# Seven products in place of eight over 1024 rather than 512 inner rows of six down projections

## The chip, the cores and the metric

One core of one Trainium2 chip runs the whole program. The metric is the device time of one execution in microseconds (us). GB/s and MB are decimal; a load of 512 KB is 0.524 MB.

## The reference, cut to what matters

Two layers work on 256 tokens of width 2048: a mixer each (attention with a window beside a gated recurrence, then stick-breaking attention), and after each mixer an MLP. The change touches the MLPs alone.

```python
def squared_relu_mlp(hn, w_up, w_down):            # hn: 256 x 2048
    return jnp.square(jax.nn.relu(hn @ w_up)) @ w_down   # w_up: 2048 x 8192, w_down: 8192 x 2048
...
h = h + squared_relu_mlp(rms_norm(h, norm_mlp[layer]), w_up[layer], w_down[layer])
```

## The kernel before

Every operand of the large matmuls is float32, split into two parts that TensorE takes at its fast rate: ScalarE writes the rounded part (`w_hi`), VectorE the rest (`w_lo` = raw - `w_hi`), and a product of two operands x and w is three matmuls, x_hi·w_hi, x_hi·w_lo and x_lo·w_hi.

Weights come in pieces of 512 KB over SyncE's queue into a ring `raw` of four slots, and their two parts go into a ring `w_split` of four slots. ScalarE splits piece v once it has landed and once TensorE is through with piece v-4; VectorE follows (`lo_done`), and then TensorE may take piece v and SyncE may load piece v+4. ScalarE and VectorE run three pieces ahead (`AHEAD = 3`): at step s of a quad or a pair they split piece s+3, and at its last three steps the first three pieces of what comes next. Each engine keeps to its written order, so an instruction that waits holds up all behind it.

An MLP is four chunks of 2048 hidden units. A chunk has four up quads (eight pieces each, 128 matmuls; four tiles of hidden units) and then the down projection of the chunk's 2048 inner rows to the 2048 output columns. When two tiles of an up quad are complete (after pieces 3 and 7) the drain `hidden` takes them: a copy `cross` on ScalarE, `total` and `relu_sq` on VectorE, a split into `ff_op` by both. In the last chunk of each layer the down projection is four plain wide quads.

In the other three chunks of each layer, six in all, it is two pairs, p = 0 and p = 1, of 1024 output columns each. A pair is an output of two row halves (tokens 0 to 127 and 128 to 255) by two column halves of 512 (n = 0, 1). A piece of a pair is (n, s): 256 inner rows s by 512 columns. Plainly it gives two products of six matmuls, one for each row half. The first two row blocks (s = 0, 1) of both column halves make a 2 by 2 by 2 block product, and it is done with seven products in place of eight, with sums of x (`x_sum`, made once a chunk) and of weights (`w_sum`). So a pair has 31 products, 186 matmuls: 24 plain ones of 12 pieces, one each of the four pieces of the block, three of sums (after pieces 5, 7 and 8). The weight sums are four VectorE instructions (`w_sum_t1`, `w_sum_t3_t2`, `w_sum_t4`) and one more copy of a piece that SyncE loads.

In `pair_dve`, VectorE does at step s: the part `w_lo` of piece s+3, then what belongs to the step; `pair_add` adds a PSUM bank, scaled by 1/rms, into `h`. Four of the eight adds come early in the pair, because an intermediate product has to go into two quarters of the output and its bank is used again.

GpSimd issues four DMAs of 512 KB and a few small ones in the first mixer, and does nothing in the MLPs.

Of the kernel before, what the change touches and what calls it, by code (L numbers as in the profile page):

```python
# [29 lines left out]
F32 = mybir.dt.float32  # L30
F32R = mybir.dt.float32r
# [5 lines left out]
P = 128  # L37
# [8 lines left out]
GC = 256  # L46
# [4 lines left out]
SPLIT_SLOTS = 4  # L51

# [46 lines left out]
def build(nc, x, rel_bias, norm_mix, even_w_in, even_conv_w, even_conv_b, even_gate_a_w, even_gate_a_b,  # L99
# [30 lines left out]
    with ctx:  # L130
# [26 lines left out]
        rstd_tok = rstd_all[:, S:S + TB]  # L157
        ident = sb("ident", [P, P])
# [135 lines left out]
        w_copy_in, w_sums, w_sum_hi, w_sum_lo = sem("w_copy_in"), sem("w_sums"), sem("w_sum_hi"), sem("w_sum_lo")  # L294
# [363 lines left out]
        def norm_sum(dve, n):  # L658

            dve.wait_ge(sq_done_tok, 8 * (n + 1))  # L660
            if n % 2:
# [6 lines left out]
                dve.wait_ge(rstd_done, n + 1)  # L668
                return
# [724 lines left out]
        SUM_AT = (0, 1, 0)  # L1394

        def after_pair(Q, v):

            return 10 * Q + (v + 1 if v < 9 else 11 if v == 9 else v + 2 if v < 15 else 20)

        def after_pair_half(Q, n, tb):  # L1400

            return 10 * Q + (10 + tb if n == 0 else 17 + 3 * tb)

        def pair_banks(p):

            return 1 + 2 * p, 2 * p, 2 - 2 * p, 3 - 2 * p

        def load_pair(sp, Q, w, row, col, T):

            for v, (n, s) in enumerate(PAIR):  # L1410
                slot = v % RAW_SLOTS
                if v not in (AT_B11, AT_B21):
                    sp.wait_ge(lo_done, 8 * Q + (v + 1 if v + 1 in (AT_B11, AT_B21) else v) - RAW_SLOTS + 1)
                src = w[bass.ds(row + s * 2 * P, 2 * P), bass.ds(col + n * 2 * GC, 2 * GC)].rearrange("(t p) n -> p t n", p=P)
                sp.dma_start(rows_512(raw[:, slot]), src).then_inc(raw_in[slot], 16)
                if v == AT_B11:
                    src = w[bass.ds(row, 2 * P), bass.ds(col + 2 * GC, 2 * GC)].rearrange("(t p) n -> p t n", p=P)
                    if not (isinstance(T, int) and T == 0):
                        sp.wait_ge(w_sum_lo, 3 * T - 1)
                    sp.dma_start(w_sum[:, 1], src).then_inc(w_copy_in, 16)  # L1420

        def x_sums_dve(dve, C, U):
# [4 lines left out]
            s1, s2, s3, s4 = (x_sum[:, i].rearrange("p (t n) -> p t n", t=2) for i in range(4))  # L1427
            dve.tensor_tensor(s1, a21, a22, ALU.add).then_inc(x_sums, 1)
            dve.tensor_tensor(s3, a11, a21, ALU.subtract).then_inc(x_sums, 1)
            dve.wait_ge(x_sums, 4 * C + 1)  # L1430
            dve.tensor_tensor(s2, s1, a11, ALU.subtract).then_inc(x_sums, 1)
            dve.wait_ge(x_sums, 4 * C + 3)
            dve.tensor_tensor(s4, a12, s2, ALU.subtract).then_inc(x_sums, 1)

        def x_sums_split(which, eng, C):

            if which == "act":
                eng.wait_ge(x_sums, 4 * C + 4)
                if not (isinstance(C, int) and C == 0):
                    eng.wait_ge(sum_pe, 6 * C)  # L1440
                eng.activation(x_sum_op[:, :, 0], x_sum[:], ACT.Copy).then_inc(x_sum_hi, 1)
            else:
                eng.wait_ge(x_sum_hi, C + 1)
                eng.tensor_tensor(x_sum_op[:, :, 1], x_sum[:], x_sum_op[:, :, 0].bitcast(F32), ALU.subtract).then_inc(x_sum_lo, 1)

        def w_sum_t1(dve, Q, T):
# [407 lines left out]
```

## Time and profile before

| | |
|---|---|
| median of three runs | 2083.76 us (2083.52 to 2084.83) |
| the profiled execution | 2083.83 us, its span 2082.1 us |
| TensorE busy in the span | 2071.0 us, 99% |
| VectorE, ScalarE, GpSimd busy | 1385.3, 1062.2, 51.7 us |
| granted clock of TensorE | 0.999 of full speed |
| DMA | 397.40 MB, 191 GB/s over the span |

The profile is of one execution. TensorE's matmuls overlap in the trace: each is shown for about 0.39 us, while the next one starts about 0.23 us after it, so the distance of starts is the pace, not the length. In a timeline a row is start, length, engine, line, instruction, destination and sources, count, and in brackets the idle time before it and what ended it.

### The profile page before, as it was taken

The page shows a single profiled execution, that of the slowest core. Times are in us where ns is not written, and L with a number is a line of the kernel's source. Part 1 is how long each engine was busy: PE and PEld are TensorE (multiplying, and loading weights), DVE is VectorE, ACT ScalarE, POOL GpSimd, SP SyncE. Part 2 cuts the span into 40 slices and gives each one's busy share as a digit, 9 for nine tenths or more (in the row PEclk, how much of TensorE's full clock was granted, in tenths as well). Part 3 has the DMA queues.
Part 4 walks back from the last instruction along what each step waited for, and adds up shares of the span by engine and source line. Part 5 has one row for each costly group of instructions (what it writes and reads, how often), then busy time and mean ns, then how long its engine had stood idle before and what let it go on. Part 6 is the DMA issues. An engine that isn't in the chain of part 4 may idle for free.

```text
span 2082.1 us, 30055 instructions
## 1 busy us (share of the span) xinstructions
PE 2071.0 (99%) x10743; PEld 1756.3 (84%) x10743; DVE 1385.3 (67%) x1757; ACT 1062.2 (51%) x1454; POOL 51.7 (2%) x95
## 2 busy tenths in 40 slices
PE   9999999999999999999999999999999999999998
PEld 8888888888888888888888888888888888888886
DVE  6798566776876686655546666566766776785654
ACT  7589555444544554544444444455544544554454
POOL 3010000000000000000000000000000000000000
PEclk9999999999999999999999999999999999999999
DMA  8544655666666566565665554556666666566654
GB/s 269 177 143 150 205 183 181 223 202 186 197 214 191 190 211 194 183 199 184 189 193 183 162 166 150 185 176 205 200 203 184 207 210 188 190 218 206 197 192 146
DMA packets 299196, 397.40 MB, mean 191 GB/s; under 512 B 12464, under 2 KB 201552, under 8 KB 298960
## 3 DMA queue, kind: packets, MB, share of 16 engines
q1 hardware_dynamic: 297872, 392.01, 60.0%
q0 software_dynamic: 944, 3.70, 0.6%
q8 instruction: 64, 1.05, 0.2%
q14 instruction: 44, 0.36, 0.1%
q10 hardware_dynamic: 272, 0.29, 0.0%
HBM read 393.82 MB, written 2.12 MB: 190 GB/s over the span
## 4 chain that ended last, share of the span: by engine, by line
PE 96%; DVE 1%; ACT 1%; issue 1%; DMA 0%; DVEq 0%; ACTq 0%
PE psum L405 49%; PE psum L1568 7%; PE psum L1570 7%; PE psum L1569 7%; PE psum L451 7%; PE psum L452 7%; PE psum L453 7%; PE psum L426 1%; PE psum L485 1%; PE psum L1113 0%; DVE w_split L1495 0%; DVE w_sum L1456 0%; PE psum L1269 0%; PE psum L1311 0%; ACT w_split L1490 0%
## 5 line engine op out<-in xcount | busy, mean ns | idle before, releaser
L405 PE MATMUL psum<-hg_op,w_split 128*128 128x512 f32 (+1 forms) x5888 | 1035.7, 337 | 0.0
L405 PEld LDWEIGHTS psum<-hg_op,w_split 128*128 128x128 f32 x5888 | 895.6, 188 | 133.6 <-issue 2.9
L384 DVE TENSOR_TENSOR w_split<-raw,w_split 128x1024 fp32r<-128x1024 f32 x518 | 630.8, 1226 | 480.8 <-ACT w_split L377 474.7
L377 ACT ACTIVATE w_split<-raw 128x1024 fp32r<-128x1024 f32 x518 | 544.9, 1058 | 539.6 <-PE psum L405 334.7
L1490 ACT ACTIVATE w_split<-raw 128x1024 fp32r<-128x1024 f32 x180 | 189.2, 1057 | 175.6 <-PE psum L1570 133.5
L1495 DVE TENSOR_TENSOR w_split<-raw,w_split 128x1024 fp32r<-128x1024 f32 x180 | 216.8, 1221 | 87.8 <-ACT w_split L1490 87.8
L1568 PE MATMUL psum<-w_split,ff_op 128*128 128x512 f32 x624 | 243.4, 390 | 0.0
L1570 PE MATMUL psum<-w_split,ff_op 128*128 128x512 f32 x624 | 243.2, 390 | 0.0
L1569 PE MATMUL psum<-w_split,ff_op 128*128 128x512 f32 x624 | 242.9, 389 | 0.0
L451 PE MATMUL psum<-w_split,ff_op 128*128 128x512 f32 x496 | 194.4, 392 | 0.5 <-DVE w_split L384 0.5
L453 PE MATMUL psum<-w_split,ff_op 128*128 128x512 f32 x496 | 193.1, 389 | 0.0
L452 PE MATMUL psum<-w_split,ff_op 128*128 128x512 f32 x496 | 193.0, 389 | 0.0
L1570 PEld LDWEIGHTS psum<-w_split,ff_op 128*128 128x128 f32 x624 | 117.1, 188 | 25.0
L1569 PEld LDWEIGHTS psum<-w_split,ff_op 128*128 128x128 f32 x624 | 117.1, 188 | 24.8
L1568 PEld LDWEIGHTS psum<-w_split,ff_op 128*128 128x128 f32 x624 | 117.1, 188 | 24.8
L451 PEld LDWEIGHTS psum<-w_split,ff_op 128*128 128x128 f32 x496 | 93.2, 188 | 19.6 <-DVE w_split L384 0.9
L453 PEld LDWEIGHTS psum<-w_split,ff_op 128*128 128x128 f32 x496 | 93.1, 188 | 19.5
L452 PEld LDWEIGHTS psum<-w_split,ff_op 128*128 128x128 f32 x496 | 93.2, 188 | 18.8
L466 ACT ACTIVATE cross<-psum 128x256 f32<-128x256 f32 x188 | 66.0, 379 | 56.0 <-PE psum L405 54.4
L550 ACT ACTIVATE ff_op<-relu_sq 128x256 f32 (+1 forms) x128 | 48.5, 418 | 86.0 <-DVE relu_sq L555 85.7
L471 DVE TENSOR_TENSOR total<-psum,cross 128x256 f32<-128x256 f32 x188 | 74.1, 418 | 24.6 <-ACT cross L466 23.9
L1510 DVE SCALAR_TENSOR_TENSOR h<-psum,rstd,h 128x512 f32<-128x512 f32 x96 | 69.6, 744 | 0.7 <-issue 0.3
(200 smaller groups left out, 1411.1 us busy)
## 6 DMA issues: line engine op xcount, KB each, us to landing
raw<-in_w_up_dram SPq DMA_DIRECT2D x256, 512.0 KB, 3.8
raw<-in_w_down_dram SPq DMA_DIRECT2D x256, 512.0 KB, 4.6
raw<-in_odd_w_in_dram SPq DMA_DIRECT2D x96, 512.0 KB, 3.6
raw<-in_even_w_in_dram SPq DMA_DIRECT2D x56, 512.0 KB, 4.5
raw<-in_even_w_out_dram SPq DMA_DIRECT2D x32, 512.0 KB, 3.8
raw<-in_odd_w_out_dram SPq DMA_DIRECT2D x32, 512.0 KB, 3.8
w_sum<-in_w_down_dram SPq DMA_DIRECT2D x12, 512.0 KB, 6.1
early_r<-rel_dram POOLq DMA_DIRECT2D x4, 512.0 KB, 6.2
```

The costliest lines, as they stand in the source:

```text
L377: act.activation(w_hi[:, slot], raw[:, rs], ACT.Copy).then_inc(hi_done, 1)
L384: dve.tensor_tensor(w_lo[:, slot], raw[:, rs], w_hi[:, slot].bitcast(F32), ALU.subtract).then_inc(lo_done, 1)
L405: ins = nc.tensor.matmul(o, l, r, start=(k == 0 and n == 0), stop=(k == KT - 1 and n == 1), skip_group_check=True)
L451: nc.tensor.matmul(acc, xh, hi[:, kt], start=(k == 0), stop=False)
L452: nc.tensor.matmul(acc, xh, lo[:, kt], start=False, stop=False)
L453: ins = nc.tensor.matmul(acc, xl, hi[:, kt], start=False, stop=(k == KT - 1))
L471: dve.tensor_tensor(total[:, i], psum[:, i, 0:S], cross[:, i], ALU.add).then_inc(bank_free, 1)
L1490: eng.activation(rows_512(w_hi[:, slot]), src, ACT.Copy).then_inc(hi_done, 1)
L1495: eng.tensor_tensor(rows_512(w_lo[:, slot]), src, rows_512(w_hi[:, slot]).bitcast(F32), ALU.subtract).then_inc(lo_done, 1)
L1568: nc.tensor.matmul(psum[:, bank], xh[:, kt], hi[:, kt], start=first and kt == 0, stop=False, skip_group_check=True)
L1569: nc.tensor.matmul(psum[:, bank], xh[:, kt], lo[:, kt], start=False, stop=False, skip_group_check=True)
L1570: ins = nc.tensor.matmul(psum[:, bank], xl[:, kt], hi[:, kt], start=False, stop=kt == 1, skip_group_check=True)
```

## The change

The seven-product identity covers the row blocks s = 0 to 3 of a pair, as two block products q = 0, 1 (q takes the row blocks 2q and 2q+1), in all six chunks. The signs differ, so that three of the four weight sums are plain additions, and those are made by DMAs that add their source to what stands in SBUF (`accum_op=ALU.add`), issued from GpSimd: six adding loads and two plain ones a pair. One sum of each block (U = B12 + B11) stays on VectorE. The order of the pieces (`PAIR`), the banks and the places of the adds are new. A product whose sign turned is added with -1/rms (`minus_rstd_tok`, one small instruction for each MLP). `x_sum` shares the memory of `w_sum` and is now made after up quads 0 and 1 and split in quads 1 and 2; up quads 1 and 2 are written out in place of a loop, and SyncE's loop over chunks is unrolled.

```diff
+SUM_SLOTS = 3
-        x_sum = sb("x_sum", [P, 4, S])
         w_sum = sb("w_sum", [P, 2, 2, 2 * GC])
+        x_sum_op = sb("x_sum_op", [P, 2, 2, 4, S], F32R)
+        w_sum_op = sb("w_sum_op", [P, SUM_SLOTS, 2, 2, 2 * GC], F32R)
...
-        PAIR = [(1, 0), (0, 0), (0, 2), (0, 3), (1, 1), (0, 4), (0, 5), (0, 1), (0, 6), (0, 7)] + [(1, s) for s in range(2, 8)]
-        AT_T1, AT_B11, AT_B22, AT_B21 = 0, 1, 4, 7
-        SUM_AFTER = {5: 0, 7: 1, 8: 2}
+        PAIR = [(1, 0), (0, 0), (1, 2), (0, 2), (1, 4), (1, 1), (1, 5), (1, 3), (1, 6), (0, 1), (1, 7), (0, 3)] + [(0, s) for s in range(4, 8)]
+        AT_U, AT_B11, AT_B22, AT_B21 = (0, 2), (1, 3), (5, 7), (9, 11)
+        SUM_AFTER = {6: (0, 1), 8: (2, 3), 12: (4,), 13: (5,)}
+        SUM_SPLIT = {2: (0,), 4: (1,), 5: (2,), 7: (3,), 8: (4,), 9: (5,)}
...
+        def sums_pool(pool, layer, c):
+            wd, Q0 = w_down[layer], (Q_MLP0, Q_MLP1)[layer]
+            for p in range(2):
+                T, Q = 2 * ((CHUNKS - 1) * layer + c) + p, Q0 + 8 * c + 4 + 2 * p
+                for q in range(2):
+                    if T:
+                        pool.wait_ge(w_sum_lo, 6 * T - 3 + q)
+                    pool.dma_start(w_sum3[q], piece(wd, D * c, 1024 * p, 1, 2 * q)).then_inc(w_sum3_in[q], 16)
+                for q in range(2):
+                    pool.wait_ge(w_sum3_in[q], 32 * T + 16)
+                    pool.dma_start(w_sum3[q], piece(wd, D * c, 1024 * p, 1, 2 * q + 1), accum_op=ALU.add).then_inc(w_sum3_in[q], 16)
+                for q in range(2):
+                    pool.wait_ge(lo_done, 8 * Q + AT_U[q] + 1)
+                    pool.dma_start(w_sum[:, q], piece(wd, D * c, 1024 * p, 1, 2 * q + 1), accum_op=ALU.add).then_inc(w_add_in[q], 16)
+                for q in range(2):
+                    pool.wait_ge(w_sum_lo, 6 * T + q + 1)
+                    pool.dma_start(w_sum[:, q], piece(wd, D * c, 1024 * p, 0, 2 * q + 1), accum_op=ALU.add).then_inc(w_add_in[q], 16)
...
+        def w_sum_u(dve, Q, q):
+            b12, b11 = AT_U[q], AT_B11[q]
+            dve.wait_ge(raw_in[b12], 16 * (2 * Q + 1))
+            dve.wait_ge(raw_in[b11], 16 * (2 * Q + 1))
+            dve.tensor_tensor(w_sum[:, q], rows_512(raw[:, b12]), rows_512(raw[:, b11]), ALU.add).then_inc(w_sums, 1)
...
         def w_sum_split(which, eng, T, j):
+            kind, q = divmod(j, 2)
+            src = w_sum3[q] if kind == 1 else w_sum[:, q]
+            slot = j % SUM_SLOTS
             if which == "act":
+                if kind == 1:
+                    eng.wait_ge(w_sum3_in[q], 32 * T + 32)
+                else:
+                    eng.wait_ge(w_add_in[q], 32 * T + 16 + 8 * kind)
+                if not (isinstance(T, int) and T == 0 and j < SUM_SLOTS):
+                    eng.wait_ge(sum_pe, 6 * T + j - SUM_SLOTS + 1)
...
         def pair_split(which, eng, Q, T, p, v):
             else:
-                if v == AT_T1:
-                    w_sum_t1(eng, Q, T)
+                if v in AT_U:
+                    w_sum_u(eng, Q, AT_U.index(v))
...
         def pair_dve(dve, Q, T, p, ahead):
             for s in range(16):
                 if s < 16 - AHEAD:
                     pair_split("dve", dve, Q, T, p, s + AHEAD)
                 else:
                     ahead("dve", dve, s + AHEAD - 16)
+                if s == 1:
+                    dve.wait_ge(pe_count, after_pair(Q, AT_U[1]))
+                    pair_add(dve, 0, n1, B, rstd_tok, part_added, 1)
                 if s == 2:
+                    dve.wait_ge(pe_count, after_pair(Q, AT_B11[1]))
+                    pair_add(dve, 0, n0, A, rstd_tok, part_added, 1)
                 if s == 7:
+                    dve.wait_ge(sum_pe, 6 * T + 2)
+                    dve.wait_ge(part_added, 4 * T + 1)
+                    pair_add(dve, 0, n1, A, minus_rstd_tok, part_added, 1)
+                if s == 9:
+                    dve.wait_ge(sum_pe, 6 * T + 4)
+                    pair_add(dve, 1, n1, A, minus_rstd_tok, part_added, 1)
+                for j in SUM_SPLIT.get(s, ()):
+                    w_sum_split("dve", dve, T, j)
...
-                up(c, 0, hook, True, sums=True)
-                with eng.Fori(1, 3) as g:
-                    up(c, g)
-                up(c, 3, sums_hook, ahead=pair_split_of(0))
+                up(c, 1, sums_hook(0), sums=True)
+                up(c, 2, sums_hook(1))
+                up(c, 3, ahead=pair_split_of(0))
```

In the new order pieces 0, 1, 2, 3, 5, 7, 9 and 11 give one product each and the other eight give two; the sums j = 0, 1 follow piece 6, j = 2, 3 piece 8, j = 4 piece 12 and j = 5 piece 13. That is 30 products, 180 matmuls. TensorE takes a sum's product only after `w_sum_lo` has counted it.

## Rows read from the trace of the kernel before

**Rows 1.** The page: busy time of the engines, and the chain that ended last.
```profile
PE 2071.0 (99%) x10743; PEld 1756.3 (84%) x10743; DVE 1385.3 (67%) x1757; ACT 1062.2 (51%) x1454; POOL 51.7 (2%) x95
...
PE 96%; DVE 1%; ACT 1%; issue 1%; DMA 0%; DVEq 0%; ACTq 0%
```

**Rows 2.** What TensorE waited for in the whole span: us in total, times, longest.
```profile
PE psum L1568 <- DVE w_split L1495: 0.9, 4, 0.2
```

**Rows 3.** TensorE's timeline: first product of a second pair, and what follows its last.
```profile
594.80 0.39 PE L1568 MATMUL psum<-w_split,x_sum_op 128*128 128x512 f32 x1
...
637.15 3.18 PE L405 MATMUL psum<-hg_op,w_split 128*128 128x512 f32 x17
```

**Rows 4.** TensorE's timeline in the third chunk's first pair (start, length).
```profile
726.32 0.40 PE L1568 MATMUL psum<-w_split,x_sum_op 128*128 128x512 f32 x1
...
734.30 0.39 PE L1570 MATMUL psum<-w_split,ff_op 128*128 128x512 f32 x1
734.90 0.50 PE L1568 MATMUL psum<-w_split,x_sum_op 128*128 128x512 f32 x1 [0.21 <-DVE w_split L1495]
```

**Rows 5.** The timeline of VectorE around the start of that chunk's two pairs.
```profile
717.61 0.75 DVE L471 TENSOR_TENSOR total<-psum,cross 128x256 f32<-128x256 f32 x2
718.27 0.75 DVE L555 SCALAR_TENSOR_TENSOR relu_sq<-total 128x256 f32<-128x256 f32 x2
...
719.85 1.22 DVE L1449 TENSOR_TENSOR w_sum<-raw 128x1024 f32<-128x1024 f32 x1
722.27 1.22 DVE L1495 TENSOR_TENSOR w_split<-w_sum,w_split 128x1024 fp32r<-128x1024 f32 x1 [1.20 <-ACT w_split L1490]
723.41 1.22 DVE L1495 TENSOR_TENSOR w_split<-raw,w_split 128x1024 fp32r<-128x1024 f32 x1
...
725.97 0.42 DVE L471 TENSOR_TENSOR total<-psum,cross 128x256 f32<-128x256 f32 x1
...
727.28 0.75 DVE L555 SCALAR_TENSOR_TENSOR relu_sq<-total 128x256 f32<-128x256 f32 x2
...
729.47 1.23 DVE L1495 TENSOR_TENSOR w_split<-raw,w_split 128x1024 fp32r<-128x1024 f32 x1 [0.52 <-ACT w_split L1490]
730.61 0.74 DVE L1510 SCALAR_TENSOR_TENSOR h<-psum,rstd,h 128x512 f32<-128x512 f32 x1
731.27 1.22 DVE L1454 TENSOR_TENSOR w_sum<-raw,w_sum 128x1024 f32<-128x1024 f32 x1
...
770.48 1.23 DVE L1495 TENSOR_TENSOR w_split<-raw,w_split 128x1024 fp32r<-128x1024 f32 x1 [0.17 <-ACT w_split L1490]
```

**Rows 6.** The timeline of ScalarE over the same stretches.
```profile
721.18 1.06 ACT L1490 ACTIVATE w_split<-w_sum 128x1024 fp32r<-128x1024 f32 x1 [1.70 <-DVE w_sum L1449]
...
727.73 0.75 ACT L550 ACTIVATE ff_op<-relu_sq 128x256 fp32r<-128x256 f32 x2 [0.82 <-DVE relu_sq L555]
728.39 2.94 ACT L1490 ACTIVATE w_split<-raw 128x1024 fp32r<-128x1024 f32 x3
...
770.76 1.07 ACT L1490 ACTIVATE w_split<-raw 128x1024 fp32r<-128x1024 f32 x1 [0.31 <-PE psum L1570]
```

**Rows 7.** Landing times: the down projections' loads (L1415), the extra copy (L1420).
```profile
DMA to landing us min/median/max: 3.5/4.7/6.7
...
DMA to landing us min/median/max: 5.7/6.1/7.1
```

**Rows 8.** GpSimd's plain 512 KB DMAs: issue in ns, and landing.
```profile
L792 POOL DMA_DIRECT2D early_r<-rel_dram x4: 761/780/817, 26.4 to 106.7; - x4
...
DMA to landing us min/median/max: 4.2/6.2/7.6
```

**Rows 9.** Stretches: engines busy (x instructions), granted clock, share of the DMA engines, GB/s.
```profile
716.00:718.00 2.00, 2.00 (x14) 1.73 (x13) 1.53 (x3) 0.98 (x3) 0.00 (x0) 1.00 1.02 373
...
726.32:769.18 42.86, 42.65 (x187) 34.84 (x186) 32.90 (x36) 20.52 (x22) 0.00 (x0) 1.00 0.65 213
769.18:811.70 42.52, 42.52 (x188) 35.07 (x187) 31.23 (x31) 19.75 (x19) 0.00 (x0) 1.00 0.68 208
```

More of the change, by code:

```diff
@@ L1404, in pair_banks, with piece, load_pair @@
         def pair_banks(p):
-            return 1 + 2 * p, 2 * p, 2 - 2 * p, 3 - 2 * p
-        def load_pair(sp, Q, w, row, col, T):
+            return ((1, 0, 3, 2), (2, 0, 3, 1))[p]
+        def piece(w, row, col, n, s):
+            return w[bass.ds(row + s * 2 * P, 2 * P), bass.ds(col + n * 2 * GC, 2 * GC)].rearrange("(t p) n -> p t n", p=P)
+        def load_pair(sp, Q, w, row, col):
             for v, (n, s) in enumerate(PAIR):
                 slot = v % RAW_SLOTS
[L1412 to L1420, printed above, removed]
@@ L1422, in x_sums_dve @@
-        def x_sums_dve(dve, C, U):
+                sp.wait_ge(lo_done, 8 * Q + v - RAW_SLOTS + 1)
+                sp.dma_start(rows_512(raw[:, slot]), piece(w, row, col, n, s)).then_inc(raw_in[slot], 16)
+        def sums_pool(pool, layer, c):
[15 more added lines that the diff above has]
+                    pool.dma_start(w_sum[:, q], piece(wd, D * c, 1024 * p, 0, 2 * q + 1), accum_op=ALU.add).then_inc(w_add_in[q], 16)
@@ L1475, in pair_split @@
         def pair_split(which, eng, Q, T, p, v):
             slot = v % SPLIT_SLOTS
-            src = w_sum[:, 0] if v == AT_T1 else rows_512(raw[:, slot])
+            src = w_sum[:, AT_U.index(v)] if v in AT_U else rows_512(raw[:, slot])
             if which == "act":
-                if v == AT_T1:
-                    eng.wait_ge(w_sums, 4 * T + 1)
+                if v in AT_U:
+                    eng.wait_ge(w_sums, 2 * T + AT_U.index(v) + 1)
                 else:
@@ L1574, in x, with sum_of_x @@
                 return ff_op[:, k:k + 2, tb * P:(tb + 1) * P], ff_op[:, k:k + 2, S + tb * P:S + (tb + 1) * P]
-            def sum_of_x(i):
-                return tuple(x_sum_op[:, i, part].rearrange("p (t n) -> p t n", t=2) for part in range(2))
+            def sum_of_x(q, i):
+                return tuple(x_sum_op[:, q, part, i].rearrange("p (t n) -> p t n", t=2) for part in range(2))
             def ring(v):
@@ L1690, in mlp @@
             chunk_by_sums(0, both(norm_hook(nrm), turn_hook(nrm, 3, Q0 - 1)))
-            with eng.Fori(1, CHUNKS - 1) as c:
-                chunk_by_sums(c, None)
+            if which == "sp":
+                for c in range(1, CHUNKS - 1):
+                    chunk_by_sums(c, None)
+            else:
+                with eng.Fori(1, CHUNKS - 1) as c:
+                    chunk_by_sums(c, None)
             c = CHUNKS - 1
@@ L1807, in _ @@
             stick_const_pool(pool)
+            for c in range(CHUNKS - 1):
+                sums_pool(pool, 0, c)
             for n in range(NF):
                 stick_pool(pool, n)
+            for c in range(CHUNKS - 1):
+                sums_pool(pool, 1, c)
             gain_pool(pool)
```

185 lines of the change are left out of this document (82 added, 103 removed).

## The prediction

> **What bounds the kernel now.** I read the page first: TensorE is busy 2071.0 of 2082.1 us and makes 96% of the chain that ended last [rows 1]. So time comes off only with matmuls, and is lost only where TensorE waits. Then its waits: on the pairs' `w_lo` parts it idles 0.9 us in the whole span, in four places [rows 2]. Then its pace, from the distance of starts: a second pair takes 637.15 - 594.80 = 42.35 us for 186 matmuls, 0.2277 us each [rows 3], so a product of six takes 1.37 us. That is the figure to keep: shown lengths of 0.39 us would promise 70% more. Last, how near VectorE is to it: its busy time is the third figure after the length of a stretch, 32.9 of 42.86 us in a first pair and 31.2 of 42.52 us in a second, 77% and 73% [rows 9]. A first pair already has a short stall: piece 4 starts 0.60 us after the matmul before it, where 0.23 is the pace, so 0.37 us are lost to VectorE [rows 4].
>
> **What is removed.** 186 - 180 = 6 matmuls a pair, 12 pairs, 72 x 0.2277 = **16.4 us**.
>
> **What VectorE has to do.** Before, a pair gives it 16 parts, 4 weight sums and 3 parts of sums, 23 long instructions; after it, 16 + 2 + 6 = 24. Back to back these start 1.14 us apart (722.27, 723.41), and an add takes 0.66 us until the next (730.61, 731.27) [rows 5]. 24 x 1.14 + 8 x 0.66 = 32.6 us of the 41.0 that 180 matmuls take. As a sum it fits; but the new order puts single products first, 1.37 us of TensorE against 1.14 us for the part alone, with sums and adds on top. So I walk the start of a pair.
>
> **First pair, p = 0, in the third chunk.** Until 724.55 nothing differs: VectorE makes the sum U for piece 0 at 719.85, ScalarE splits it 1.33 later (721.18), VectorE's part of piece 0 is at 722.27 (1.09 after ScalarE's start), that of piece 1 at 723.41 [rows 5, 6]. Now piece 2 is a sum too. Its U runs 724.55 to 725.77; ScalarE +1.33 = 725.88; VectorE's part +1.09 = 726.97 to 728.19. Before, that part was over when `total` began at 725.97. Behind it stands the drain of the up quad's last two tiles, on both engines: `total` 728.11, `relu_sq` +0.66 = 728.77 (as 717.61 to 718.27), ScalarE's split of it +0.45 = 729.22 (727.28 to 727.73), ScalarE's part of piece 3 +0.66 = 729.88 (727.73 to 728.39), VectorE's +1.08 = 730.96 (728.39 to 729.47) to 732.19 [rows 5, 6]. TensorE starts the pair at 726.32 and wants piece 3 after three single products, at 726.32 + 4.10 = 730.42; it gets it at 732.19 + 0.14 = 732.33 (0.14 is my estimate of the signal's way). **It waits 1.9 us.** Before, piece 3 came after five products and was early.
> Then VectorE is busy without a gap: piece 4 732.10, add 733.24, piece 5 733.90, add 735.04, sum j = 0 735.70, piece 6 736.84 to 738.06. TensorE wants piece 6 at 732.33 + 4 x 1.37 = 737.80 and gets it at 738.20: **0.4 us**. After that: piece 7 737.98, sum 1 739.12 to 740.3, wanted at 742.3; what follows is ready 2 us and more ahead. A stall isn't won back, since TensorE is what everything else then waits for. So 2.3 us are lost, the old 0.37 is gone: +1.93 x 6 first pairs = **+11.6 us**.
>
> **Second pair, p = 1.** No drain stands between, and the split of piece 2 waits for TensorE's last piece but one anyway. Before it, piece 3's part is at 770.48, 1.3 after the pair's start at 769.18, and ScalarE's part of piece 4 at +1.6 [rows 5, 6, 9]. Then VectorE: piece 4 2.7, add (end of piece 2, 4.35) to 5.0, piece 5 to 6.15, add 6.8, sum 0 7.95, piece 6 7.95 to 9.2; wanted at 9.6. It fits by 0.3 us: nothing, at worst 0.3 x 6 = 2 us.
>
> **The adding DMAs.** No row shows one. A plain DMA of 512 KB from GpSimd lands in 4.2 to 7.6, median 6.2 us, its issue 0.78 us included [rows 8]; SyncE's in 4.7 and 6.1 [rows 7]. An adding one also reads what it adds to: one more transfer, 0.524 MB at the 373 GB/s of a full stretch [rows 9] = 1.4 us, so I take 7.6 to 9. Below, 6.2; above, twice the plain one, 12.4. When are they wanted? For q = 0 the issue follows piece 0's part (723.5, with 0.2 for the wait), and piece 6 stands behind sum 0 on VectorE, so ScalarE must take the sum by 734.6: it may land in 10.9 us. For q = 1 it follows piece 2's part (728.2), and sum 1 is wanted at 742.3, so ScalarE at 739.8: 11.4 us. In a second pair 12.2 and 11.2 us, by the same steps. At 7.6 to 9 us all is hidden by the two pieces ahead; **0 us**. At 12.4 it costs about 1.5 us in each of 12 pairs, and each us beyond costs 12. The next two additions (sums 4, 5) are issued at about 737 and 740 and wanted after 755, the other memory's sums (j = 2, 3) are loaded a pair ahead: nothing.
> GpSimd does nothing else then; its waits are in the order in which they come true (sum 3's split of one pair before piece 0's of the next, some 16 us). SyncE loses one extra copy a pair. The 96 loads for 12 copies add 44 MB.
>
> **The small rest.** A second set of x sums, four instructions of 0.4 us and a split of 1.2 on VectorE, lies in up quads; at the end of quad 0 the same work leaves TensorE without a wait [rows 2], so 0. The written-out loop and the small factor for each MLP: 0, within 1 us either way.
>
> The sum: 2083.83 - 16.4 + 11.6 = **2079.0 us**, against the profiled execution, whose own time stands 0.07 above the median; the gap of 1.7 us around the span stays. 0.2% (4.2 us) is about what a measurement of this kernel can tell from none, and the forecast, -4.8, is hardly past it.
>
> **Rivals.**
> *The adding DMAs land late* (slower). Place: ScalarE at steps 2 and 4 of each pair, held by `w_add_in`; it decides from 11.2 us on. For it: an add to memory is a read, a second read and a write, and twice the plain time is 12.4. Against: the plain one lands in 6.2. At 12.4 us it gives 2079 + 18 = 2097, at 15 us 2079 + 12 x 3.7 = 2123.
> *The DMA engines are full* (slower or none). A pair moves 24 loads in place of 17, at 1.4 us 34 of 41 us, and if six of them cost double 42. For it: full stretches are seen at share 1.02 [rows 9]. Against: the share over a pair is 0.65 to 0.68 [rows 9], and the up quads can take what is not urgent. Landing times of 8 us for raw pieces would cost 0.5 to 1 us a pair, 2085 to 2091. The Trainium skill (DMA: Bandwidth & Descriptors, "Issuing engines are not separate DMA queues") says of this that DMAs issued by GpSimd, SyncE or ScalarE run on the same 16 engines and interleave, so that GpSimd's queue brings no bandwidth of its own. No row of before shows it, since GpSimd issues nothing in a pair; with the rule the time would be this rival's, without it 2079.0.
> *The stall at piece 3 is not there* (faster): were the drain quicker or TensorE later than walked, 16.4 us would stay whole but for 0 to 1 us: 2067.5. Against it: each step is a distance measured in the same stretch.
>
> **The numbers.** The walk as told 0.48 (2076.5 to 2081.5; past 0.2% in 0.28 of it, within in 0.20); late additions 0.27 (0.25 slower, 0.02 within); full engines 0.10, slower; no stall 0.15, faster. Faster 0.43, same 0.22, slower 0.35. The range goes from 2066 (no stall) to 2099 (additions at 12.4 us); beyond it are some 0.15, additions of 13 us and more. The likeliest case's own range is 2076.5 to 2081.5.
>
> **What would show it.** TensorE idle about 1.9 us before piece 3 and 0.4 before piece 6 in each first pair, ended by VectorE's `w_split`; none in second pairs; pairs of about 43.4 and 41.0 us. The DMA groups of GpSimd: landing under 11 us. ScalarE's waits on `w_sum<-w_down` small. Wrong it would be made by TensorE waiting on `w_sum_op` (late additions), by raw pieces landing after 7 us, or by first pairs of 41 us.

## The result and the profile after

The changed kernel takes 2131.57 us, the median of four runs (2125.17 to 2133.01), and the kernel before took 2083.64 on the same chips (four runs, 2083.49 to 2084.83): a ratio of 1.0223, 95% interval 1.0202 to 1.0244. The change costs 48 us. The profiled execution has a span of 2129.6 us, 47.5 longer than before. Its page:

```profile
PE 2072.0 (97%) x10671; PEld 1742.6 (82%) x10671; DVE 1412.2 (66%) x1801; ACT 1097.3 (52%) x1496; POOL 157.8 (7%) x191
...
q1 hardware_dynamic: 294608, 385.72, 56.4%
q0 software_dynamic: 23984, 54.03, 12.4%
...
PE 78%; DMA 10%; DVE 6%; ACT 3%; issue 2%; SPq 0%; DVEq 0%; ACTq 0%
```

The 72 matmuls are gone (10743 to 10671). VectorE and ScalarE are as idle as before. What is new stands in the chain: 96% of it was TensorE [rows 1], now 78%, and 10% is DMA, which was 0%. The waits name who held whom (us in total, times, longest). TensorE's are the two lines that start with PE; the others are of the engines before it:

```profile
ACT w_split L1508 <- DMA raw<-in_w_down_dram: 129.9, 80, 4.5
...
ACT w_split L1508 <- DVE w_sum L1474: 80.5, 23, 8.8
...
PE psum L1580 <- DVE w_split L1513: 37.1, 29, 2.9
...
DVE w_sum L1474 <- DMA raw<-in_w_down_dram: 28.3, 6, 5.8
...
PE psum L1580 <- DVE h L1528: 7.3, 7, 1.8
```

On the pairs' products TensorE waits 44.4 us (37.1 and 7.3) in place of 0.9 [rows 2]. Read one link further back: ScalarE waits 80 times for a raw piece of the ring, 129.9 us. In the kernel before it did so too, but less, and TensorE hardly felt it:

```profile
ACT w_split L1490 <- DMA raw<-in_w_down_dram: 38.5, 33, 2.7
```

For a sum that GpSimd's loads make, ScalarE waits nearly never; its 80.5 us are for VectorE's own sum U. The landing times say the same, line by line (the ring's loads, then GpSimd's additions for sums 0 and 1):

```profile
L1424 SPq DMA_DIRECT2D raw<-in_w_down_dram x192: 367/368/368, 361.7 to 1925.7; - x192
...
DMA to landing us min/median/max: 3.5/7.2/10.8
...
L1440 POOL DMA_DIRECT2D w_sum<-in_w_down_dram x24: 1194/1202/1212, 375.9 to 1903.2; - x24
...
  ACT w_sum_op L1488: 0.5, 1
...
DMA to landing us min/median/max: 8.1/9.0/10.2
```

The additions land in 9.0 us at the median, at the end of the forecast 7.6 to 9 and under the 10.9 us at which they would be late, and ScalarE waited for one of them once, 0.5 us. But the plain pieces went from a median of 4.7 us [rows 7] to 7.2. The third chunk's two pairs, in TensorE's timeline: the first starts at 743.68, the second at 789.14, the next up quad at 837.00.

```profile
743.68 0.39 PE L1580 MATMUL psum<-w_split,x_sum_op 128*128 128x512 f32 x1
...
747.61 0.40 PE L1582 MATMUL psum<-w_split,x_sum_op 128*128 128x512 f32 x1
749.70 0.50 PE L1580 MATMUL psum<-w_split,ff_op 128*128 128x512 f32 x1 [1.69 <-DVE w_split L1513]
...
757.02 0.49 PE L1580 MATMUL psum<-w_split,ff_op 128*128 128x512 f32 x1 [1.50 <-DVE w_split L1513]
...
792.67 0.50 PE L1580 MATMUL psum<-w_split,x_sum_op 128*128 128x512 f32 x1 [0.58 <-DVE w_split L1513]
...
803.71 0.50 PE L1580 MATMUL psum<-w_split,ff_op 128*128 128x512 f32 x1 [2.38 <-DVE w_split L1513]
```

All four waits are for pieces whose part was late: piece 3 at 749.70 and piece 6 at 757.02 in the first pair, pieces 2 and 6 at 792.67 and 803.71 in the second, where none was forecast. All four say "VectorE". Who was really late is seen on ScalarE and VectorE:

```profile
747.27 1.99 ACT L1508 ACTIVATE w_split<-raw 128x1024 fp32r<-128x1024 f32 x2
...
754.57 1.06 ACT L1508 ACTIVATE w_split<-raw 128x1024 fp32r<-128x1024 f32 x1 [1.71 <-DMA raw<-in_w_down_dram]
```
```profile
748.34 2.36 DVE L1513 TENSOR_TENSOR w_split<-raw,w_split 128x1024 fp32r<-128x1024 f32 x2 [0.52 <-ACT w_split L1508]
...
784.24 1.23 DVE L1474 TENSOR_TENSOR w_sum<-raw 128x1024 f32<-128x1024 f32 x1 [5.07 <-DMA raw<-in_w_down_dram]
```

At piece 3 no transfer is late: that is the drain, as walked. At piece 6 ScalarE was held 1.71 us by a raw piece. VectorE's first sum of the second pair stood 5.07 us waiting for one; that wait alone costs little, since run 5 below has six like it (25.3 us, the longest 5.1) and is hardly slower for it.

The other 7.3 us, seven waits, stand each before the product of a sum, but not because an addition is late: they are ended by VectorE adding the bank into `h`. The longest shows why. VectorE made that add behind the part of a piece whose raw data came late (TensorE, and ScalarE before it, in the program's first pair):

```profile
401.83 0.47 PE L1580 MATMUL psum<-w_sum_op,x_sum_op 128*128 128x512 f32 x1 [1.78 <-DVE h L1528]
```
```profile
398.70 1.06 ACT L1508 ACTIVATE w_split<-raw 128x1024 fp32r<-128x1024 f32 x1 [3.75 <-DMA raw<-in_w_down_dram]
```

The third chunk's two pairs as stretches, columns as in [rows 9], and then two short ones inside:

```profile
743.68:789.14 45.46, 42.10 (x182) 33.56 (x181) 33.16 (x36) 22.88 (x26) 8.35 (x8) 1.00 0.96 269
789.14:837.00 47.86, 43.98 (x181) 34.64 (x180) 33.69 (x33) 23.39 (x23) 3.99 (x4) 0.96 0.85 241
...
780.00:782.00 2.00, 2.00 (x10) 1.68 (x9) 0.00 (x0) 0.00 (x0) 0.00 (x0) 1.00 1.10 273
...
806.00:807.00 1.00, 1.00 (x4) 0.72 (x4) 1.00 (x2) 1.00 (x3) 0.09 (x1) 0.50 1.03 184
```

The pairs take 45.5 and 47.9 us, not 43.4 and 41.0. The DMA engines are busy at a share of 0.96 over a whole first pair, where it was 0.65 [rows 9], yet they move only 269 GB/s; before, a full stretch moved 373. At 780 the share is 1.10 while VectorE and ScalarE do nothing at all: TensorE lives on the pieces that are ready, and everything ahead of it waits for DMA. Last, the clock: after the 2.4 us for which TensorE stood idle before 803.71 it was granted 0.50 (the 1.2 GHz level) for some 3 us, and matmuls there start 0.43 us apart.

### The profile page after: what moved, and what is told of

Its sections match the earlier page's. It is cut to its first block, busy times and chain, and to the rows that moved or that the text cites. A ratio compares the mean times of both kernels' runs of the same rounds, so it can differ in the third digit from the quotient of the medians.

```text
span 2129.6 us, 28916 instructions
## 1 busy us (share of the span) xinstructions
PE 2072.0 (97%) x10671; PEld 1742.6 (82%) x10671; DVE 1412.2 (66%) x1801; ACT 1097.3 (52%) x1496; POOL 157.8 (7%) x191
## 3 DMA queue, kind: packets, MB, share of 16 engines
q0 software_dynamic: 23984, 54.03, 12.4%
q8 instruction: 87, 1.43, 0.3%
## 4 chain that ended last, share of the span: by engine, by line
PE 78%; DMA 10%; DVE 6%; ACT 3%; issue 2%; SPq 0%; DVEq 0%; ACTq 0%
PE psum L410 45%; DMA raw<-in_w_down_dram 9%; PE psum L456 7%; PE psum L458 7%; PE psum L457 7%; PE psum L1580 3%; PE psum L1581 3%; PE psum L1582 3%; DVE w_split L1513 3%; ACT w_split L1508 2%; DVE w_sum L1474 1%; DMA raw<-in_even_w_in_dram 1%; PE psum L490 0%; DVE h L1528 0%; ACT w_split L382 0%
## 5 line engine op out<-in xcount | busy, mean ns | idle before, releaser
L389 DVE TENSOR_TENSOR w_split<-raw,w_split 128x1024 fp32r<-128x1024 f32 x518 | 630.9, 1226 | 480.5 <-ACT w_split L382 476.1
L382 ACT ACTIVATE w_split<-raw 128x1024 fp32r<-128x1024 f32 x518 | 545.2, 1058 | 541.2 <-PE psum L410 336.5
L1508 ACT ACTIVATE w_split<-raw 128x1024 fp32r<-128x1024 f32 x168 | 176.5, 1055 | 150.8 <-DMA raw<-in_w_down_dram 129.9
L1513 DVE TENSOR_TENSOR w_split<-raw,w_split 128x1024 fp32r<-128x1024 f32 x168 | 203.7, 1222 | 67.9 <-ACT w_split L1508 67.5
L1580 PE MATMUL psum<-w_split,ff_op 128*128 128x512 f32 x480 | 191.9, 400 | 32.0 <-DVE w_split L1513 32.0
L456 PE MATMUL psum<-w_split,ff_op 128*128 128x512 f32 x496 | 194.4, 392 | 0.5 <-DVE w_split L389 0.5
L458 PE MATMUL psum<-w_split,ff_op 128*128 128x512 f32 x496 | 193.2, 389 | 0.0
L457 PE MATMUL psum<-w_split,ff_op 128*128 128x512 f32 x496 | 193.1, 389 | 0.0
L1582 PE MATMUL psum<-w_split,ff_op 128*128 128x512 f32 x480 | 189.2, 394 | 0.0
L1581 PE MATMUL psum<-w_split,ff_op 128*128 128x512 f32 x480 | 189.2, 394 | 0.0
L1580 PEld LDWEIGHTS psum<-w_split,ff_op 128*128 128x128 f32 x480 | 91.2, 190 | 61.6 <-DVE w_split L1513 28.4
L456 PEld LDWEIGHTS psum<-w_split,ff_op 128*128 128x128 f32 x496 | 93.1, 188 | 19.6 <-DVE w_split L389 0.9
L458 PEld LDWEIGHTS psum<-w_split,ff_op 128*128 128x128 f32 x496 | 93.1, 188 | 19.4
L457 PEld LDWEIGHTS psum<-w_split,ff_op 128*128 128x128 f32 x496 | 93.2, 188 | 19.0
L1582 PEld LDWEIGHTS psum<-w_split,ff_op 128*128 128x128 f32 x480 | 91.3, 190 | 20.0
L1581 PEld LDWEIGHTS psum<-w_split,ff_op 128*128 128x128 f32 x480 | 91.2, 190 | 18.8
L555 ACT ACTIVATE ff_op<-relu_sq 128x256 fp32r<-128x256 f32 (+1 forms) x128 | 48.3, 419 | 88.9 <-DVE relu_sq L560 88.9
L1440 POOL DMA_DIRECT2D w_sum<-in_w_down_dram x24 | 28.8, 1202 | 826.8 <-DVE w_split L1513 826.8
```

Of the source, the lines that this page charges most:

```text
L382: act.activation(w_hi[:, slot], raw[:, rs], ACT.Copy).then_inc(hi_done, 1)
L389: dve.tensor_tensor(w_lo[:, slot], raw[:, rs], w_hi[:, slot].bitcast(F32), ALU.subtract).then_inc(lo_done, 1)
L456: nc.tensor.matmul(acc, xh, hi[:, kt], start=(k == 0), stop=False)
L457: nc.tensor.matmul(acc, xh, lo[:, kt], start=False, stop=False)
L458: ins = nc.tensor.matmul(acc, xl, hi[:, kt], start=False, stop=(k == KT - 1))
L1508: eng.activation(rows_512(w_hi[:, slot]), src, ACT.Copy).then_inc(hi_done, 1)
```

## Theories

*A: the DMA engines are full.* A load that adds keeps them busy for about twice as long as a plain one; a pair's 24 loads fill nearly the whole pair, and the ring's pieces, which stand in the same engines, come late. *B: it is the bytes* (44 MB more), adding or not. *C: it isn't the transfers*: the new order on VectorE with the drain, or the longer code of the unrolled quads, costs more than walked. C is told apart by leaving the loads out, B by making them plain.

## Experiments

Times are medians; the label of each run, by which the expectations call it, stands in brackets. The kernel before took 2083.5 to 2084.5 us beside them (2084.5 beside e1 to e4, 2083.5 beside e5 to e8), so a difference between runs of two groups is good to about 1 us.

**1. The loads by themselves (e1).** A kernel with nothing but 512 KB loads of the same shape: twelve at a time in flight, plain from SyncE, plain from GpSimd, adding from GpSimd, then twelve adding beside twelve plain, then adding ones one by one.

> The disputed cost by itself; this kernel computes nothing of the reference, it only loads pieces of 512 KB: twelve plain loads from SyncE in flight together, then twelve plain ones from GpSimd, twelve adding ones from GpSimd, twelve adding ones from GpSimd beside twelve plain ones from SyncE, then two adding and two plain ones, each alone. Theory A (an adding load holds the DMA engines about twice as long as a plain one, because its bytes are read twice): 12 plain in about 17 us from either queue, 12 adding in 30 to 35 us, 12 of each together in 45 to 52 us. Theory B (an adding load costs the engines what a plain one costs, and what hurts is the number of bytes): 17, 17 and 35 us. One adding load alone: 4.5 to 6 us under A, 3.5 to 4 under B.

It took 155.9 us. The stretches, in that order (length, GpSimd's busy time, clock, share, GB/s), and two single loads on GpSimd's timeline:

```profile
10.00:15.00 5.00, 0.00 (x0) 1.00 1.05 397
30.00:35.00 5.00, 0.00 (x0) 1.00 1.02 389
55.00:75.00 20.00, 0.81 (x1) 1.00 1.12 204
90.00:120.00 30.00, 0.52 (x1) 1.00 1.10 262
```
```profile
127.99 1.22 POOL L126 DMA_DIRECT2D buf<-in_w_down_dram  x1 [37.47 <-DMA buf<-in_w_down_dram]
134.10 1.20 POOL L126 DMA_DIRECT2D buf<-in_w_down_dram  x1 [4.89 <-DMA buf<-in_w_down_dram]
```

At full share, plain loads move 397 GB/s and adding ones 204. A load of 0.524 MB takes 0.524 / 397 = 1.32 us of all sixteen engines plain (1.35 from GpSimd) and 2.57 us adding. Theory A had said 30 to 35 us for twelve adding loads; 12 x 2.57 is 31. Alone, an adding load lands 5.8 us after its issue, and a plain one from SyncE 3.6:

```profile
DMA to landing us min/median/max: 5.8/5.8/5.9
```
```profile
DMA to landing us min/median/max: 3.6/3.6/3.6
```

So it is slower by 2.2 us also when nothing stands beside it (no plain load from GpSimd was run alone). The Trainium skill (Collectives: The Full Stack, "The bandwidth ceiling: the fold count and why AG ≠ RS ≠ AR") says of ReduceScatter, a reduction between cores, that it is slower than a copy because the add needs two source reads, and gives a measured ratio of 1.93. The 397 / 204 = 1.95 here (1.91 against GpSimd's plain loads) agrees, for loads into one core; that the second read is the reason here no run shows.

With the measured 1.35 and 2.57, a pair needs 18 x 1.35 + 6 x 2.57 = 39.7 us of the engines, and has 41.0.

**2. Without the loads (e2).** All of the change but GpSimd's eight loads a pair and their waits; sums are split from whatever stands there.

```diff
-            for p in range(2):
-                T, Q = 2 * ((CHUNKS - 1) * layer + c) + p, Q0 + 8 * c + 4 + 2 * p
...
+            return
```

> The changed kernel with none of GpSimd's 96 loads: each sum is split from whatever stands in its buffer, so the products of sums are of other numbers, and all instructions of TensorE, VectorE and ScalarE stay. Theory A or B (the loads of the sums fill the DMA engines, and raw pieces land late): the time of the walk in the prediction, 2079 us (2076 to 2082), with TensorE idle only before piece 3 (1.9 us) and piece 6 (0.4 us) of first pairs. Theory C (the new order overloads VectorE and ScalarE by itself): above 2110 us.

2086.22 us (2085.02 to 2087.27), ratio 1.0009 (1.0000 to 1.0019). The loads are worth 2131.6 - 2086.2 = 45.4 us: nearly all of the loss. But 2086.2 is not 2079 either, nor in the expected 2076 to 2082. TensorE's waits, the ring's landing, and the turn from the second pair to the next chunk, each of this kernel:

```profile
PE psum L1562 <- DVE w_split L1495: 9.8, 6, 1.7
```
```profile
DMA to landing us min/median/max: 3.5/4.6/5.8
```
```profile
637.18 2.02 PE L410 MATMUL psum<-hg_op,w_split 128*128 128x512 f32 x10 [1.29 <-DVE h L1510]
```

Six waits of up to 1.7, one for each first pair, and none in second pairs: the walk stands. The ring lands as before the change. In place of the seamless 637.15 [rows 3] the up quad begins after a gap of 1.29 us. A like one of 1.46 stands at 1723.90, in the second layer, and one of 1.33 at 1727.95, inside the quad that follows.

**3. Plain loads in place of adding ones (e3).** The same bytes, issued at the same places; the sums are only their last term. Of the three places with an adding load one is shown.

```diff
-                    pool.dma_start(w_sum[:, q], ..., accum_op=ALU.add).then_inc(w_add_in[q], 16)
+                    pool.dma_start(w_sum[:, q], ...).then_inc(w_add_in[q], 16)
```

> The changed kernel with plain loads in place of the 72 adding ones: same bytes from memory, same queue, same places, but what they load is not added, so the sums are other numbers. Theory A (adding is what fills the engines): 24 loads at 1.4 us are 34 of 41 us, so most of the loss goes: 2083 to 2095 us. Theory B (the bytes do it): 2125 to 2132 us as now.

2091.59 us (2089.33 to 2092.12), ratio 1.0031 (1.0020 to 1.0043). GpSimd's queue and the ring's landing:

```profile
q0 software_dynamic: 14768, 54.03, 8.0%
```
```profile
DMA to landing us min/median/max: 3.6/6.0/9.5
```

The bytes cost 5.4 us (from 2086.2), the adding 40.0 (to 2131.6). B falls. The queue's share shows the size again: the same 54.03 MB take 12.4% of 2129.6 = 264 us of the engines when they add and 8.0% of 2089.9 = 167 when they don't, 97 / 72 = 1.35 us more for each of 72 adding loads, and in 128 more packets each ((23984 - 14768) / 72).

**4 and 5. Half of the loads (e4, e8).** Which half costs? Either only the four into `w_sum`, issued while the pair runs (e4, whose main cut is shown), or only the four into the separate memory, two plain and two adding, ready long ahead (e8, where the other two loops over q are left out instead).

```diff
-                for q in range(2):
-                    pool.wait_ge(w_sum3_in[q], 32 * T + 16)
-                    pool.dma_start(w_sum3[q], ..., accum_op=ALU.add).then_inc(w_sum3_in[q], 16)
```

> The changed kernel without the four loads a pair of the separate memory (two plain, two adding); the four adding loads into w_sum stay. The sums j = 2, 3 are split from another buffer, so their products are of other numbers. Theory A: 16 x 1.4 + 4 x 2.8 = 34 of 41 us of the engines, near the result with plain loads: 2083 to 2097 us. If instead the loss were that sums 0 and 1 come late (their additions are the ones kept), it would stay near 2125 us.

> The changed kernel with only the four loads a pair of the separate memory (two plain, two adding), which are issued from 16 us after a pair's start on, when TensorE takes a piece each 2.7 us; the four early adding ones into w_sum are left out, and the sums split from w_sum are of other numbers. DMA engines: 18 x 1.35 + 2 x 2.56 = 29.4 of 41 us. Theory A with the place counted (an adding load hurts when pieces that give one product are being fetched, 1.37 us each): near e2_no_loads, 2087 to 2091 us, while e4_half_loads with the early ones took 2105.5. If only the sum of engine time counted, e8 would cost as much as e4: 2100 to 2105 us.

e4: 2105.46 us (2103.66 to 2106.69), ratio 1.0094 (1.0074 to 1.0114), so +19.2. e8: 2086.61 us (2083.73 to 2088.36), ratio 1.0011 (1.0002 to 1.0021), so +0.4. e4 lies above its expected 2083 to 2097, e8 just under its 2087 to 2091. Apart the halves cost 19.6, together 45.4, so there is no fixed price per load. e8 also shows that two adding loads a pair can be free. But e4 does not fit a mere sum of engine time: by 1.35 and 2.57 it needs 31.9 us a pair and costs 19.2, while run 3 needs 32.4 and costs 5.4. Its four adding loads are all issued in the first half of the pair, where the single products stand; whether it is the place or the adding that hurts there, beyond the sum, is not separated. Waits of TensorE in e4 and then in run 3:

```profile
PE psum L1571 <- DVE w_split L1504: 17.0, 10, 3.2
PE psum L1571 <- DVE h L1519: 8.2, 7, 1.7
```
```profile
PE psum L1580 <- DVE w_split L1513: 11.6, 8, 1.7
```

**6. The drain behind the pieces (e5)**, on top of run 2. VectorE makes the second sum U ahead of its part of piece 1, in place of piece 2, and before first pairs the up quad's last split of `ff_op` stands behind piece 3's on both engines.

```diff
+                if s == 0 and drain_rest:
+                    drain_rest("dve", dve)
...
-                if v in AT_U:
-                    w_sum_u(eng, Q, AT_U.index(v))
+                if v < 2:
+                    w_sum_u(eng, Q, v)
```

> The changed kernel without GpSimd's loads (sums of other numbers, as in e2_no_loads), and with the start of the first pair reordered: the second sum U is made before the part of piece 1, and of the up quad's last two tiles only cross, total and relu_sq stand before the split of piece 3, their split into ff_op behind it. Theory of the walk (the 1.9 us before piece 3 and the 0.4 us before piece 6 come from what stands before those parts on VectorE and ScalarE): both waits go, 6 x 2.3 = 13.7 us below e2_no_loads, 2072 to 2074 us. If they came from something else, 2086 us as e2_no_loads.

2073.74 us (2073.05 to 2075.14), ratio 0.9950 (0.9934 to 0.9967): 12.5 less than run 2 (11.5 if each is taken against the kernel before beside it), where the walk gives 6 x (1.9 + 0.4) = 13.8. What is left of the wait:

```profile
PE psum L1570 <- DVE w_split L1499: 0.3, 1, 0.3
```

**7. The loop over chunks written out (e6)**, on top of run 2, without the edit of run 6. Theory C in its second form: the gaps at 637.18, 1723.90 and 1727.95 are the loop's.

```diff
-                with eng.Fori(1, CHUNKS - 1) as c:
-                    chunk_by_sums(c, None)
+            for c in range(1, CHUNKS - 1):
+                chunk_by_sums(c, None)
```

> The changed kernel without GpSimd's loads (sums of other numbers), and with the loop over the middle chunks written out on all engines. e2_no_loads has three gaps of 1.4 to 1.7 us on TensorE at the turns of that loop (before the first matmul of an up quad and inside one), which the kernel before does not have. Theory: they are the jump of a loop whose body the change has made longer by writing out two up quads; without a jump they go: 2086.2 - 5 = 2081 us. Rival: they are waits on PSUM banks, as the trace writes them down; then 2086 us as e2_no_loads.

2080.00 us (2079.54 to 2081.24), ratio 0.9982 (0.9973 to 0.9992): 6.2 less than run 2 (5.2 against the kernels before beside them). The gaps themselves make 4.1 us, 4.9 with the 0.27 that each costs beyond what is shown (below); the wait before piece 3 is also 0.17 us shorter in four of the six first pairs. The same place in TensorE's timeline has no gap:

```profile
635.68 0.39 PE L1564 MATMUL psum<-w_split,ff_op 128*128 128x512 f32 x1
635.91 3.29 PE L410 MATMUL psum<-hg_op,w_split 128*128 128x512 f32 x18
```

**8. A whole version with fewer adding loads (e7).** With both repairs, and the first two sums of each pair made by VectorE from the ring (its slot is held until then); four adding loads a pair are left.

```diff
+                if v - RAW_SLOTS in AT_B22:
+                    sp.wait_ge(w_t2, 2 * T + AT_B22.index(v - RAW_SLOTS) + 1)
...
+                if s in T2_AT:
+                    dve.tensor_tensor(w_sum[:, q], w_sum[:, q], rows_512(raw[:, slot]), ALU.add).then_inc(w_t2, 1)
```

> A whole version: the reordered start of e5, the loop written out as in e6, and two of the six adding loads of a pair (those of sums 0 and 1, U + B22) made by VectorE from the ring in place of a DMA, with sums 0, 1 taken after piece 7 and sums 4, 5 after pieces 13 and 14. VectorE gets 2 x 1.14 us a pair more. DMA engines: 16 + 2 plain loads at 1.35 and 4 adding at 2.56 us = 34.5 of 41 us, all four adding ones issued in the middle or late in the pair. Theory A: raw pieces 6 to 9 no longer meet adding loads, the time comes to 2070 to 2085 us, about the kernel before or under it. If any adding load costs what it cost in the change (45 us for 72, so 30 for 48): 2098 us or more.

2097.88 us (2096.66 to 2099.15), ratio 1.0065 (1.0049 to 1.0082): not the 2070 to 2085 of theory A but the number of its rival, 2098 or more. The rival's reason is not what happens, though: run 12, with as many adding loads, is 14 us faster. A stall that none had before stands at piece 1 of second pairs, because the swap of run 6 puts VectorE's second sum U, and with it the wait for its raw piece, ahead of piece 1's part (VectorE, then TensorE):

```profile
597.82 1.23 DVE L1481 TENSOR_TENSOR w_sum<-raw 128x1024 f32<-128x1024 f32 x1 [3.15 <-DMA raw<-in_w_down_dram]
```
```profile
600.24 0.50 PE L1599 MATMUL psum<-w_split,ff_op 128*128 128x512 f32 x1 [2.42 <-DVE w_split L1523]
```

**9 and 10. Sums on VectorE, the swap in first pairs only (e9, e10).** With all of `w_sum` made by VectorE from the ring (e9: two adding loads a pair are left), or only the first two sums (e10: four are left).

```diff
+                if v - RAW_SLOTS in AT_B21:
+                    sp.wait_ge(w_t4, 2 * T + AT_B21.index(v - RAW_SLOTS) + 1)
...
+                    dve.tensor_tensor(w_sum[:, q], w_sum[:, q], rows_512(raw[:, AT_B21[q] % RAW_SLOTS]), ALU.add).then_inc(w_t4, 1)
```

> A whole version: reordered start of the first pair (the second U ahead of piece 1's part in first pairs only, since in e7 it made second pairs wait for a late raw piece), the chunk loop written out, and four of the six adding loads of a pair made by VectorE from the ring: U + B22 at steps 3 and 4, then + B21 at steps 8 and 9. Left on GpSimd: two plain and two adding loads a pair into the separate memory, which cost nothing in e8. DMA engines 18 x 1.35 + 2 x 2.56 = 29.4 of 41 us; VectorE 32.6 + 4 x 1.14 = 37.2 us, 39.5 in a first pair. If the DMA engines were the whole loss: 2073.7 - 6 = 2068 us and up to 2078 with small waits on VectorE's sums, 0.3 to 0.8% under the kernel before. If VectorE is now the bound at the start of pairs: above 2083 us.

> As e9, but with the additions of B21 (sums 4 and 5) by adding loads from GpSimd in the middle of the pair; it is e7 with the order of U in second pairs put back. DMA engines 34.5 of 41 us. Theory A: between e9 and e7, 2078 to 2090 us; e7's excess was partly its wait for raw pieces at the start of second pairs (some 2.5 us each, 15 us together) and partly the adding loads in the middle. If only the order of U was at fault: as e9 within 2 us.

Both missed. e9: 2124.96 us (2122.07 to 2126.55), ratio 1.0194 (1.0179 to 1.0208); e10: 2097.97 us (2094.37 to 2098.82), ratio 1.0061 (1.0045 to 1.0077). Putting the order of U back in second pairs (e10) gained nothing over run 8: the stall has only moved from piece 1 to piece 2 of the same pair.

```profile
603.90 0.50 PE L1601 MATMUL psum<-w_split,x_sum_op 128*128 128x512 f32 x1 [3.02 <-DVE w_split L1525]
```

The DMA engines are relieved in e9, but see SyncE's queue there, and what follows from it on ScalarE:

```profile
SPq L1433 <- DVE w_sum L1574: 121.5, 24, 8.2
SPq L1431 <- DVE w_sum L1570: 68.0, 24, 4.4
```
```profile
ACT w_split L1517 <- DMA raw<-in_w_down_dram: 175.7, 65, 11.6
```

SyncE's loads are issued in order, so a slot that is held for a later sum (up to 8.2 us) holds every load behind it. I had counted VectorE's instructions and not what they hold. VectorE's own load has also grown, and neither run tells the two apart.

**11. All adding loads, both repairs (e11).** If stalls add up, 2131.6 - 12.5 - 6.2 = 2112.9.

> The changed kernel with all its 96 loads from GpSimd as they were, and with the two repairs that took 12.5 and 6.2 us off the version without loads: the reordered start of first pairs and the chunk loop written out. Theory A: the raw pieces stay late, since the DMA engines are full for most of a pair; the repairs give back less than alone, because VectorE and ScalarE wait for raw pieces there too: 2115 to 2128 us. If the losses were independent and added up: 2131.6 - 18.7 = 2113 us. Below 2100 would say that the full DMA engines were not the main cause.

2125.03 us (2121.85 to 2128.33), ratio 1.0195 (1.0179 to 1.0211): the repairs give 6.5 and not 18.7, as theory A said (2115 to 2128). TensorE waits nearly as much as before them, 41.3 in place of 44.4:

```profile
PE psum L1593 <- DVE w_split L1522: 41.3, 31, 2.2
```

While the raw pieces come late, a stall that is taken away turns up later in the pair. After runs 2 and 3 this is the plainest sign for A.

**12. Run 10 without VectorE's two sums and the held slot (e12).** Loads as in run 10 (four adding, two of them in the middle of the pair).

> e10_fourth_sum_on_dma without the two VectorE sums from the ring (U + B22) and without the wait of SyncE for them; sums 0 and 1 are split from U, so their products are of other numbers. All GpSimd loads, two plain and four adding a pair, stay as in e10. Two theories for the 30 us by which e10 missed: the DMA engines (34.5 of 41 us, adding loads in the middle of a pair), then it stays at 2093 to 2098 us; or the ring, whose slots the sums hold while SyncE's queue waits in order, and VectorE's two more instructions at the start of a pair, then 2070 to 2080 us. Between them the split is read off directly.

2083.96 us (2079.95 to 2089.37), ratio 1.0001 (0.9992 to 1.0011), between the two theories. So the held slots and VectorE's sums, which this run takes away together, are 14.0 of run 10's excess. Against 2086.2 - 12.5 - 6.2 = 2067.5, what both repairs would give without any load if they add up, 16.5 us are left, for the loads (the sums' new places were not tried by themselves).

**The runs side by side.** The share of the DMA engines over the twelve pairs of each profiled execution (windows from pair start to pair end, as in [rows 9]), and the cost against the same kernel without GpSimd's loads:

| loads of GpSimd in a pair | share | cost, us |
|---|---|---|
| none (run 2) | 0.64 | 0 |
| two plain and two adding, late (run 5) | 0.80 | 0.4 |
| eight plain (run 3) | 0.86 | 5.4 |
| four adding, early and mid (run 4) | 0.87 | 19.2 |
| two plain and four adding (run 12, other order) | 0.90 | 16.5, against 2067.5, which is a sum |
| two plain and six adding (the change) | 0.96 | 45.4 |

The cost starts between 0.80 and 0.86 and grows steeply; at nearly one share it is 5.4 or 19.2, so the share says where trouble begins and not what it costs. The engines are busy 44.4 us a pair in the change, more than the 39.7 worked out; the share itself reads 1.02 to 1.12 when they are full (run 1).

No whole version beat the kernel before; the best are runs 8 and 10, at 2098. The 2073.7 and 2080.0 leave sums out.

## Why the prediction was wrong

**The step that failed** is the price of "The DMA engines are full". Its own working has the number: 24 loads at 1.4 us are 34 of 41 us, "and if six of them cost double 42". They cost 1.95 times (run 1), 39.7 of 41.0 us. I then priced it at 0.5 to 1 us a pair and gave it 0.10, on the argument that the share over a pair was 0.65, and the sum had 0 for it. That share was the state without these loads. The prediction's own sign of being wrong, raw pieces landing after 7 us, is what came. Measured: 45.4 us over 12 pairs, 3.8 us a pair; 5.4 for the bytes and 40.0 for the adding (runs 2 and 3). The raw pieces did not land in 8 us, as priced, but at a median of 7.2, and even so cost four times the higher price: I took a landing time for the wait, where the load of the engines in the pair (0.97 by this count, 0.96 in the trace) and the lateness of single pieces (up to 10.8 us) were the thing to look at.

**The adding DMAs, "0 us".** Their own landing was right at the edge: 9.0 us, never above 10.2 for the first two sums, no wait of weight. The rival with the greater chance (late additions) did not happen. What I asked was whether the additions come in time; what mattered was whom they delay. The ring has little to spare: a piece's load is issued when its slot's part is done, four parts earlier, 4 x 41 / 16 = 10.2 us on average; less ScalarE's and VectorE's work on it (2.3 us) this leaves some 7.9, and less where single products stand. A median of 4.7 passes, one of 7.2 with a tail to 10.8 doesn't. That is worked out, not shown by a run of its own.

**The walk of first pairs** was right. TensorE takes piece 3 6.02 us after the pair's start (743.68, 749.70), where the walk had 6.01. The wait there was forecast as 1.9; 749.70 is 2.09 after the matmul before it, 1.86 more than the pace, and the next one is 0.10 late: 1.96. (In the first chunk of each layer it is some 0.17 less.) At piece 6, 0.4 forecast; in run 2, without the loads, it is 0.25 + 0.10. Taking them away gives 12.5 of 13.8 (run 6). With the loads, piece 6 is 1.67 late, by a raw piece. **Second pairs, 0**: right without the loads (run 2), wrong with them.

**The small rest, "0, within 1 us".** In run 2 the loop over chunks has gaps on TensorE, one at its turn in each layer and one soon after the second; writing it out gives 6.2 us (run 7). That the written-out quads are to blame, since they made the body longer, is argued, not shown: the old loop with the new pairs was not run. Code fetches went from 64 packets, 1.05 MB, to 87 and 1.43; but run 7 fetches 81 and 1.33 and has no gaps, so it is not the amount alone.

**What makes up the 47.5 us of span**, from rows of the profile after: -16.4 for the matmuls (their count and the pace); +43.5 of shown waits (44.4 - 0.9); +9.7, since each of these 36 costs 0.27 more than is shown (1.96 against 1.69, and the same at 757.02); some 4 for the clock (0.997 of 2129.6 against 0.999 of 2082.1, each rounded); 6.2 for the loop, taken from run 7. Together 47.0, but the fit is partly luck. This trace has only two gaps at the loop, of 0.99 and 0.90 us, so 2.4 and not 6.2. By stretches, the twelve pairs take 556.7 us in place of 511.2, 45.5 more, and all the rest 2.0 more. Some 4 to 5 us of the pairs are thus in no shown wait; pieces that come a little late are part of it, like the one at 799.66, 0.30 behind the pace. The clock is a cost of the second order: after some of the long waits it fell, and that costs again. It was 0.999 in runs 2 and 3, 0.995 in run 11 and 0.993 in run 9.

**Still open:** how much of run 12's 16.5 us is the two adding loads in mid pair and how much the sums' new places; why run 4 costs more than run 3 at nearly the same share; how much of runs 9 and 10 is held slots and how much VectorE; and whether a ring of more slots would let the change pay. None of these was tried.

## What to carry to other kernels

Before work is moved to DMA, sum up the engines' time of the stretch, old loads and new, with an adding load at twice a plain one. Here a share of 0.80 was nearly free, 0.86 to 0.90 cost 5 to 19 us and 0.96 cost 45, and the urgent loads, not the new ones, were late. The share says when to worry and not how much: which loads stand beside the urgent ones counts as well. Ask of each new transfer not only whether it comes in time, but what stands in the same engines beside it and how much slack that has. When stalls taken away at one place return at another (runs 10 and 11), look for what all of them wait on.

## What the runs showed of the hardware

- An adding load of 512 KB occupies the sixteen DMA engines for 2.57 us against 1.32 to 1.35 for a plain one (204 against 389 to 397 GB/s); mixed half and half 262 GB/s (run 1). Alone it lands in 5.8 us, a plain one from SyncE in 3.6. GpSimd issues it in 1.20 us, a plain one in 0.72 to 0.75.
- After standing idle 2.4 us before 803.71, TensorE was granted the 1.2 GHz level for some 3 us, beginning about a microsecond after it had resumed; after 1.7 and 1.5 us in the pair before it stayed at 2.4 GHz. The length of the one wait does not decide it: after 2.06 us before 439.13 it fell at once, after 2.07 before 621.51 and 2.27 before 1549.90 it stayed.
- Without GpSimd's loads (run 2), the changed kernel's loop over chunks had three gaps of 1.3 to 1.5 us on TensorE, at and just after its turns, which the kernel before has not; with the loop written out (run 7) they were gone and the time was 6.2 us less.
- With GpSimd's loads beside them, SyncE's 512 KB loads of the ring landed at a median of 6.0 us (eight plain ones a pair, run 3) and 7.2 (six of them adding), in place of 4.6 without (run 2).
